# Layer 0's two attention runs joined into one pipeline, and six rows' squares at the turn streamed over weights of ones

## What is computed

```python
def _rms_norm(x, g, eps=1e-6):
    y = x * lax.rsqrt(jnp.mean(x * x, axis=-1, keepdims=True) + eps)
    return y * g
...
def _diff_attend(q, k, v, lam):          # 4 heads, two maps of width 32 per head, values of 64
    s = jnp.einsum('bhcqd,bhckd->bhcqk', q, k) * (A_DQK ** -0.5)
    p = jax.nn.softmax(s, axis=-1)
    w = p[:, :, 0] - lam * p[:, :, 1]
    return jnp.einsum('bhqk,bhkd->bhqd', w, v)
...
    yA_lat = _diff_head_out(_diff_attn_blocks(qA, kA_all, vA_all, lam), g_subln_l, lam_init)  # 1280 keys
    if last: return y_lat, None
    yA_ctx = _diff_head_out(_diff_attend(_heads_qk(pc[4]), kA_ctx, vA_ctx, lam), ...)          # 256 keys
...
        h_lat = h_lat + gf * _rms_norm(f_lat, g_post_ffn[l])       # end of layer l
        h_ctx = h_ctx + gf_c * _rms_norm(f_ctx, g_post_ffn[l])
        u_lat = _modulate(_rms_norm(h_lat, g_pre_mix[l + 1]), sm, cm)   # start of layer l + 1
```

## Time and profile before

| | us |
|---|---|
| median of three runs | 3106.45 |
| lowest, highest | 3102.74, 3108.12 |
| the profiled execution's own time | 3101.55 |
| span of the profile | 3099.8 |
| TensorE busy | 2863.0 (92%) |
| VectorE busy | 1947.9 (63%) |
| ScalarE busy | 1235.6 (40%) |
| GpSimd busy | 564.8 (18%) |

### The profile page before, as it was taken

One profiled execution on the slowest core, in us unless ns is written; L12 is line 12 of the kernel. 1 busy time (PEld: TensorE's weight loads), 2 busy tenths in 40 slices (PEclk: granted clock), 3 DMA queues, 4 the chain that ended last, 5 costly groups with the idle time before them and its releaser, 6 DMA issues.

```text
span 3099.8 us, 47110 instructions
## 1 busy us (share of the span) xinstructions
PE 2863.0 (92%) x17730; PEld 1611.3 (52%) x17730; DVE 1947.9 (63%) x2717; ACT 1235.6 (40%) x2368; POOL 564.8 (18%) x449
## 2 busy tenths in 40 slices
PE   6999887889889999999998999988889999999997
PEld 4555644654535556757755554554554444444443
DVE  5976786882575405626746687678964673374755
ACT  5112455883543213313334311448864542231332
POOL 0031010001317202102212004010003161221221
PEclk9999996999999999999999799999999999999998
DMA  6111114332142111111141311113322432111142
GB/s 242 55 35 45 28 46 139 128 134 66 55 146 74 61 41 41 43 40 55 42 150 41 142 48 41 38 49 110 114 82 88 134 118 68 48 61 49 58 150 105
DMA packets 69172, 248.95 MB, mean 80 GB/s; under 512 B 9104, under 2 KB 9872, under 8 KB 69008
## 3 DMA queue, kind: packets, MB, share of 16 engines
q1 hardware_dynamic: 67856, 241.44, 23.1%
q10 hardware_dynamic: 1152, 5.24, 0.4%
HBM read 221.75 MB, written 19.92 MB: 78 GB/s over the span
## 4 chain that ended last, share of the span: by engine, by line
PE 63%; issue 19%; DVE 11%; ACT 5%; POOL 1%; DMA 1%; SPq 0%; POOLq 0%; DVEq 0%; ACTq 0%
PE PS L831 38%; PE PS L990 18%; DVE wlo L1959 2%; PE PS L852 2%; DVE R L2138 1%; ACT whi L1454 1%; DVE R L2125 1%; PE PS L1216 1%; ACT SW L1822 1%; ACT X L1573 1%; ACT R L1571 1%; DVE X L2454 1%; PE PS L1261 1%; PE PS L1195 0%; DVE X L2098 0%
## 5 line engine op out<-in xcount | busy, mean ns | idle before, releaser
L831 PE MATMUL PS<-R,whi 128*128 128x512 f16 (+1 forms) x4992 | 1354.8, 359 | 40.3 <-DVE wlo L1959 23.4
L831 PE MATMUL PS<-R,wlo 128*128 128x512 f16 (+1 forms) x2496 | 895.4, 359 | 0.0
L831 PEld LDWEIGHTS PS<-R,whi 128*128 128x128 f16 x4992 | 489.2, 99 | 537.5 <-issue 37.9
L990 PE MATMUL PS<-R,whi 128*128 128x256 f16 (+2 forms) x2352 | 510.3, 326 | 0.0
L1959 DVE SCALAR_TENSOR_TENSOR wlo<-stage,whi 128x1024 f16<-128x1024 f32 (+1 forms) x204 | 279.0, 1368 | 358.6 <-ACT whi L1454 357.6
L831 PEld LDWEIGHTS PS<-R,wlo 128*128 128x128 f16 x2496 | 245.8, 98 | 241.3 <-issue 8.5
L990 PE MATMUL PS<-R,wlo 128*128 128x256 f16 (+2 forms) x1176 | 319.2, 326 | 0.0
L990 PEld LDWEIGHTS PS<-R,whi 128*128 128x128 f16 x2352 | 230.1, 98 | 152.0
L1454 ACT ACTIVATE whi<-stage 128x1024 f16<-128x1024 f32 (+1 forms) x204 | 210.3, 1031 | 136.6 <-PE PS L831 85.0
L2164 DVE TENSOR_REDUCE tiny<-PS 128x1 f32<-128x1280 f32 (+1 forms) x144 | 197.0, 1368 | 38.6 <-PE PS L1018 38.3
L1988 DVE TENSOR_TENSOR X<-X,PS 128x256 f32<-128x256 f32 (+2 forms) x294 | 150.8, 548 | 92.6 <-PE PS L990 92.3
(11 more groups left out here) (231 smaller groups left out, 3565.5 us busy)
## 6 DMA issues: line engine op xcount, KB each, us to landing
stage<-in_w_gu SPq DMA_DIRECT2D x120, 512.0 KB, 3.4
X<-in_w_ada SPq DMA_DIRECT2D x70, 512.0 KB, 3.3
stage<-in_w_down SPq DMA_DIRECT2D x48, 512.0 KB, 3.3
stage<-in_w_in SPq DMA_DIRECT2D x44, 512.0 KB, 3.3
stage<-in_w_out SPq DMA_DIRECT2D x32, 512.0 KB, 3.2
h_save<-R SPq DMA_DIRECT2D x24, 640.0 KB, 5.3
R<-h_save SPq DMA_DIRECT2D x24, 640.0 KB, 4.7
R<-in_w_ada SPq DMA_DIRECT2D x16, 512.0 KB, 13.2
```

The source lines that it names most:

```text
L831: last = mm(slot(into, t0, t1)[:, c0 - t0:c1 - t0], w[:, j, k, :], row, start=(k == 0 and q == 0), stop=(k == K - 1 and q == 2))
L990: last = mm(s_bank(nf, t, o, n), w[:, j, k0 + k, :], row, start=(k == 0 and x == 0), stop=(k == PAIRS - 1 and x == 2))
```

## The change

Two parts.

The two runs of layer 0's attention become one pipeline of ten tiles. `attend(l)` is called once; `tile_back` and `back` make the last context tile the one before the first latent tile, `first_tile` is true only for the first tile of the layer, and `through` counts semaphores over the border (a negative head number lies in the context run). The drain after the context run, TensorE's wait for its output and the short first latent tile are gone; the first latent scores are issued within the last context tile. Layer 1's order of work is as before. SP's and GpSimd's programs are not touched.

At the turn, `turn_sums` takes the squares of h's rows 0 to 5 as the moving operand over weights of ones (two matmuls of 512 and 256 columns a row, accumulated in PSUM where the spread goes later), which puts the sum of a token on all partitions. Rows 6 and 7 are done as before. VectorE's `turn_mean_square` waits for row 5, multiplies by the identity, reduces it to a value for each token, scales it and, when row 7 is done, adds the sums of rows 6 and 7. Besides, `keep_clock(n, 6)` issues n matmuls of 256 f16 columns into bank 6, which nothing reads: 8 behind the sums of Y (in both layers), 6 behind the first columns, 8 behind the sums of h and 16 behind the second spread. They wait for nothing.

```diff
+        SPREAD_ROWS = KD - 2
...
-        def back(r, h, n):
-            return (r, h - n) if h >= n else (r - 1, HA + h - n)
+        def per_head(name, nk):
+            return {"scores": 2, "exps": 2, "wt_ps": len(key_groups(nk)), "wt": len(key_groups(nk)),
+                    "pv": len(key_groups(nk))}.get(name, 1)
+        def first_tile(l, run, r):
+            return isinstance(r, int) and r == 0 and run == attend_runs(l)[0][0]
+        def tile_back(l, run, r):
+            return ("c", CT - 1) if run == "l" and isinstance(r, int) and r == 0 else (run, r - 1)
+        def back(l, run, r, h, n):
+            return (run, r, h - n) if h >= n else tile_back(l, run, r) + (HA + h - n,)
+        def through(l, run, name, n):
+            if isinstance(n, int) and n < 0:
+                return heads_before(l, run, name) + n * per_head(name, CT) if (l, run) == (0, "l") else None
+            return n * per_head(name, CT if run == "c" else NTILE) + heads_before(l, run, name)
...
+            def keep_clock(n, bank):
+                for _ in range(n):
+                    mm(PS[:, bank, 0:2 * P], ones16[:, 0:P], ones16[:, :], start=True, stop=True)
...
-            def end_sums(k, then=None):
+            def turn_sums(k, then):
 
                 inst, a0, a1 = STEPS[k]
-                ready, used, n = ("y_sq_ready", "y_sq_used", Y_STEPS.index(STEPS[k])) if inst % 2 else \
-                    ("h_sq_ready", "h_sq_used", H_STEPS.index(STEPS[k]))
-                rows = (0, KD - 1) if inst % 2 else range(KD)
-                for d in rows:
-                    if inst % 2 and d == 0:
-                        pe.wait_ge(S[used], (KD - 1) * n + KD - 2)
+                n = H_STEPS.index(STEPS[k])
+                for d in range(KD):
+                    pe.wait_ge(S["h_sq_ready"], KD * n + d + 1)
+                    if d < SPREAD_ROWS:
+                        at = spread_to(k)
+                        for c0, c1 in spans(a0, a1):
+                            last = mm(PSF[:, at + c0 - a0:at + c1 - a0], ones[:, :], square_row(d)[:, c0:c1],
+                                      start=(d == 0), stop=(d == SPREAD_ROWS - 1))
                     else:
-                        pe.wait_ge(S[ready], KD * n + d + 1)
-                    src = xrow(2 + d % 2 if d else 0)
+                        for x in range((a1 - a0) // P):
+                            last = mm(PS[:, 7, x:x + 1], square_row(d)[:, a0 + x * P:a0 + (x + 1) * P], ones[:, 0:1],
+                                      start=(d == SPREAD_ROWS and x == 0), stop=(d == KD - 1 and x == (a1 - a0) // P - 1))
+                    if d:
+                        last.then_inc(S["h_sq_used"], 1)
+                    then(d)
+            def end_sums(k):
+                inst, a0, a1 = STEPS[k]
+                n = Y_STEPS.index(STEPS[k])
+                for d in (0, KD - 1):
+                    if d:
+                        pe.wait_ge(S["y_sq_ready"], KD * n + KD)
+                    else:
+                        pe.wait_ge(S["y_sq_used"], (KD - 1) * n + KD - 2)
                     for x in range((a1 - a0) // P):
-                        last = mm(PS[:, 7, x:x + 1], src[:, a0 + x * P:a0 + (x + 1) * P], ones[:, 0:1],
-                                  start=(d == 0 and x == 0), stop=(d == KD - 1 and x == (a1 - a0) // P - 1))
-                    if d:
-                        last.then_inc(S[used], 1)
-                    if then:
-                        then(d)
+                        last = mm(PS[:, 7, x:x + 1], square_row(d)[:, a0 + x * P:a0 + (x + 1) * P], ones[:, 0:1],
+                                  start=(d == 0 and x == 0), stop=(d > 0 and x == (a1 - a0) // P - 1))
+                last.then_inc(S["y_sq_used"], 1)
...
-            def attend(l, run, t_first, nt, nk):
-                s, before = (lambda n: S[n]), (lambda n: heads_before(l, run, n))
-                groups = key_groups(nk)
-                NG, keys, done = len(groups), nk * P, tiles_before(l, run)
...
+                def tile(run, r):
+                    first = first_tile(l, run, r)
+                    end = isinstance(r, int) and r == runs[run][1] - 1
+                    after = ("l", 0) if run == "c" and end else (run, r + 1)
+                    last = run == "l" and end
+                    done = tiles_before(l, run)
...
-                            scores(*((r, h + 1) if h < HA - 1 else (r + 1, 0)), 0, back(r, h, 1) if h or not first else None)
+                            scores(*((run, r, h + 1) if h < HA - 1 else after + (0,)), 0, back(l, run, r, h, 1) if h or not first else None)
...
-                scores(0, 0, 0)
-                tile(0, first=True)
-                if nt > 2:
-                    with pe.Fori(1, nt - 1) as r:
-                        tile(r)
-                tile(nt - 1, last=True)
-                modulation_end(nt - 1, HA - 1)
+                nt = runs["l"][1]
+                if "c" in runs:
+                    scores("c", 0, 0, 0)
+                    for r in range(runs["c"][1]):
+                        tile("c", r)
+                else:
+                    scores("l", 0, 0, 0)
+                tile("l", 0)
+                with pe.Fori(1, nt - 1) as r:
+                    tile("l", r)
+                tile("l", nt - 1)
+                modulation_end("l", nt - 1, HA - 1)
...
-                for run, t_first, nt, nk in attend_runs(l):
-                    attend(l, run, t_first, nt, nk)
-                    pe.wait_ge(S["ot_done"], tiles_before(l, run) + nt)
+                attend(l)
+                pe.wait_ge(S["ot_done"], (l + 1) * NTILE - (CT if l == LAYERS - 1 else 0))
...
                 k = step_of(4 * l + 3, 1)
                 end_sums(k)
+                keep_clock(8, 6)
                 pe.wait_ge(S["slot_free"], unit0(l + 1, "in"))
                 spread(k)
                 if l < LAYERS - 1:
                     first_columns(l + 1, 0, KD)
-                    end_sums(k + 1, lambda d: first_columns(l + 1, KD + d, KD + d + 1))
+                    keep_clock(6, 6)
+                    turn_sums(k + 1, lambda d: first_columns(l + 1, KD + d, KD + d + 1))
+                    keep_clock(8, 6)
                     spread(k + 1)
+                    keep_clock(16, 6)
...
+                    act.wait_ge(S["wt_ps"], count(run, "wt_ps", n) + (p + 1))
+                    if p:
                         if not (isinstance(r, int) and n == 0):
 
-                            act.wait_ge(s("pv"), (NG * n + (p + 1 - (NG if p else 2 * NG))) + before("pv"))
+                            act.wait_ge(S["pv"], count(run, "pv", n - 1) + (p + 1))
+                    elif not (first_tile(l, run, r) and h < 2):
+                        act.wait_ge(S["pv"], count(run, "pv", n - 2) + 1)
...
+            def turn_mean_square(k):
+                inst, a0, a1 = STEPS[k]
+                n = (a1 - a0) // P
+                used, at = (KD - 1) * H_STEPS.index(STEPS[k]), spread_to(k)
+                spread_rows = xrow(1)[:, a0:a1].rearrange("p (t c) -> p t c", c=P)
+                dve.wait_ge(S["h_sq_used"], used + SPREAD_ROWS - 1)
+                own.link(TT(spread_rows, PSF[:, at:at + a1 - a0].rearrange("p (t c) -> p t c", c=P),
+                            ident[:, :].rearrange("p (t c) -> p t c", t=1).to_broadcast([P, n, P]), ALU.mult))
+                own.link(RED(per_tok[:, 1, 0:n], spread_rows, AX.X, ALU.add))
+                own.link(TS(per_tok[:, 1, 0:n], per_tok[:, 1, 0:n], 1.0 / D, 1e-6, ALU.mult, ALU.add))
+                dve.wait_ge(S["h_sq_used"], used + KD - 1)
+                STT(per_tok[:, 0, 0:n], PS[:, 7, 0:n], 1.0 / D, per_tok[:, 1, 0:n], ALU.mult, ALU.add).then_inc(S["mean_sq"], 1)
...
-                    inverse_root(k + 1)
+                    turn_mean_square(k + 1)
+                    diagonal(k + 1)
                     scale_rows(k + 1)
```

More of the change, by code:

```diff
@@ L1057, in token_major, with modulation @@
                     last.then_inc(S["o_ps"], 1)
-                def modulation(r, h):
+                def modulation(run, r, h):
                     for x, i in enumerate(ada_step(l, run, h)):
@@ L1652, in tile @@
                         if h or not first:
-                            wt_copy(*back(r, h, 1), 0)
-                        exps(r, h, 1)
-                per = HA
-                tile(0, first=True)
+                            wt_copy(*back(l, run, r, h, 1), 0)
+                        exps(run, r, h, 1)
+                per, nt = HA, runs["l"][1]
+                for r in range(runs["c"][1] if "c" in runs else 0):
+                    tile("c", r)
+                tile("l", 0)
                 with act.Fori(1, nt) as r:
```

307 lines of the change are left out of this document (155 added, 152 removed).

## The result

The changed kernel took 3081.07 us (median of 4 runs, 3078.61 to 3083.51) beside 3105.06 for the kernel before (3102.74 to 3108.12). The ratio is 0.9921, 95% interval [0.9909, 0.9933]: 24.5 us faster, 20.8 to 28.3. The forecast was 3089.7, a gain of 16.8. The sign and the two places were right and the size was a third too small: the time lies 0.6 us inside the low end of the stated range (3080.5), and the gain is above the 23.6 that the sum gave with every term in full. The profiled execution took 3078.61 (span 3076.8), 22.9 less than that of before.

What follows compares the result with a forecast made beforehand. TensorE, busy 92% of the span, was taken as the bound. Joint 6.0, turn 10.3 and end 0.5 gave 16.8 off the profiled 3101.55, 3084.7; the median's 4.9 carried made 3089.7 us, range 3080.5 to 3099.5.

Steps and rivals of the forecast that it cites:

- First latent maximum 12.9 earlier, less 3.7 for a full tile: Layer 0's joint: drain and refill removed, 12.9 us; a full first latent tile returns 3.7, so 9.2 saved.
- 2.1 for the lower clock and 1.1 for a quarter of a further head: Layer 0's joint: first latent head 8.1 instead of 6.0; quarter of another head's 4.4 charged; 6.0 us left saved.
- The discount of 3.2: Layer 0's joint: lower clock and quarter of a further head together, taking the saving from 9.2 to 6.0 us.
- The ring, 0.6: First latent head: second modulation unit's transfer lands at 503.0, TensorE comes at 502.4 and waits 0.6 us.
- The waits, passed over: Attention's waits: SP's transfers and GpSimd's powers said to wait on the same counts; no gain was counted.
- the premise that only joint, turn and end matter: Whole kernel: no other stage of a layer moves by over 2 us, else the premise is wrong.
- The statistic 8.0 earlier: Turn into layer 1: with streamed squares the statistic is done near 1719.3 against 1727.27, 8.0 us saved.
- The weighing of the rule: Turn's squares: rule makes twelve loads 1.28 us at either clock, little gain; the forecast went by the trace, 1.50 and 2.56.
- Fillers 2.3 and end 0.5: Matmuls over ones: 2.3 us returned at the turn's spreads and first products, 0.5 at layer 1's end.
- Rows at 1.2 GHz (1): Turn: streamed rows run at 1.2 GHz, 3.35 against 3.01 us each; total gain 4.0, 3102.4; chance 0.10.
- further heads at 1.2 GHz (2 and 3): Layer 0's joint: 1.2 GHz for two further heads, 3097.3, chance 0.10; or through two latent tiles, 3124, chance 0.04.
- a drain that stays (4): Layer 0's joint: a wait still drains the pipeline, joining brings nothing; gain 10.8, 3095.6; chance 0.06.

Runs made afterwards that it cites:

- waits alone: Kernel before with only the sums in the attention's waits reordered, so that several waits share a register: 3100.72 us, ratio 0.9987.
- fillers alone: Kernel before with only 8, 6, 8 and 16 matmuls over ones added, its squares' loads as they were: 3102.34 us, ratio 0.9996.
- loads with fillers: Kernel before, squares still as twelve loads a row, with the change's matmuls over ones and four more behind each row: 3104.68 us, ratio 1.0006.
- part B alone: Kernel before with the changed kernel's turn (streamed squares, matmuls over ones) and the attention of before: 3096.65 us, ratio 0.9978.
- less the joining: Changed kernel with layer 0's attention as two runs again, keeping the new sums in the waits and the changed turn: 3090.35 us, ratio 0.9956.
- part A alone: Kernel before with layer 0's two attention runs as one pipeline and the rewritten waits, the turn as before: 3092.88 us, ratio 0.9968.
- A with three idle: The kernel of part A alone with three small scratch-scaling instructions added to VectorE's program at the turn: 3093.16 us, ratio 0.9965 to before.
- changed, again: The changed kernel itself, unaltered, measured again on the same chip as the other runs: 3080.22 us, ratio 0.9928 to before.
- without fillers: Changed kernel without any matmul over ones: 3081.92 us, ratio 0.9934 to before.
- more fillers: Changed kernel with 12 instead of 8 matmuls over ones before the first spread and 18 instead of 8 before the second: 3080.97 us, ratio 0.9926.
- fillers in every wait: Changed kernel with matmuls over ones in every wait of the turn (16, 10, 13 and 34): 3079.71 us, ratio 0.9924 to before.
- four rows: Changed kernel with four of the eight square rows streamed instead of six, the last four as twelve loads each: 3083.74 us, ratio 0.9937.

## Why the prediction was right, and where it was not

Each profiled execution can be cut at the same events. "To tile 1" is from VectorE's first maximum of the context run to the first maximum of the second latent tile. "Attention 0" is from the same first maximum to the first product of the out-projection. "Turn" is from the start of the first spread to the first half sums of layer 1's attention (it holds unchanged work too). Then come that attention's first six pitches and its last tile. Each is a difference of two start times:

```
                        to tile 1  attention 0   turn   six pitches 1  last tile 1
before                    62.08      248.15     443.24     141.15        19.57
waits alone               61.76      244.88     443.87     140.74        17.97
fillers alone             59.97      244.06     442.57     141.18        19.57
loads with fillers        59.75      243.60     447.18     141.16        18.05
part B alone              61.79      247.49     435.02     141.10        20.89
less the joining          61.88      243.47     436.01     139.86        17.86
part A alone              52.83      237.75     443.90     140.80        17.98
A with three idle         54.04      236.40     445.63     139.92        17.86
changed                   52.74      234.73     435.96     139.83        17.85
changed, again            51.70      234.33     436.05     139.81        17.86
without fillers           51.43      233.41     436.03     139.82        17.85
more fillers              53.82      237.91     435.40     139.85        17.85
fillers in every wait     51.35      237.89     433.48     139.87        17.86
four rows                 51.53      234.83     436.25     139.88        17.86
```

What differs between the traces of before and after: attention 0 13.4, turn 7.3, layer 1's attention 1.3 and 1.7, 23.7 in all, less 0.6 at the start. But attention 0 alone varies by 4.7 between kernels that share its structure, before's execution was the longest of its six and after's below the mean of its eight. The means are 245.3 with two runs and 235.9 with one: 9.4, and of the 13.4 some 4 are how the executions fell. The 9.4 holds some of the waits' gain: the two kernels that have two runs and the new sums average 244.2, which leaves 8.3 for the joining by itself.

**First latent maximum 12.9 earlier, less 3.7 for a full tile: right.** The eight joined executions have it 28.5 to 28.7 behind the context run's first, where 28.8 was forecast. To tile 1 the means are 52.4 and 61.2: 8.8 saved, 9.34 in the compared pair, 9.2 forecast before the discounts.

**2.1 for the lower clock and 1.1 for a quarter of a further head: the step that failed.** The events came as described, 0.50 in the first head and a wait for the ring even three times as long, yet the first latent tile took 24.15, in the mean of eight 23.85 (22.82 to 25.33), which is a steady tile. The working held the first head's 8.1 against an average head of 6.0. In this kernel's steady tile the heads are uneven: 6.32, 5.60, 6.36, 5.37 (first maxima at 570.93, 577.25, 582.85, 589.21 and 594.58). The joint's were 7.44, 5.11, 6.24, 5.36. So the first lost 1.12, not 2.1, and the next two gave 0.6 of it back; the slack that the windows of the earlier trace rows had shown on both engines is the likely reason. In four of the eight the first head took only 6.1 to 6.5. No further head came at 1.2 GHz here. In two others (more fillers, A with three idle) the clock was at 0.50 again for some 6 us in the second and third head, and the second took 6.11 and 6.25 instead of 5.11: 1.1 lost, where the forecast had up to 4.4. The discount of 3.2 should have been about 0.5.

**The ring, 0.6: mis-sized, 1.81** (1.43 to 1.88 in the eight), and hidden in the same slack. What it would be worth to have the transfer earlier was not tried.

**The waits, passed over: the term that was missing.** "SP's other transfers and GpSimd's powers keep their order and wait on the same counts" was true and beside the point: the counts of the attention were summed in another order, and several waits now share a register. That is worth 4.0 (1.2 to 6.8) by the run on it, and the premise that only joint, turn and end matter was wrong for layer 1: 3.0 us moved there, over the 2 us that was named as the test. Of its pitches 0.3 to 0.4 in all goes with the waits (140.74 and 140.80 against 141.15) and 1.0 more with where VectorE's loop stands in its program, as the three idle instructions show; with the old waits, in part B alone, VectorE's longer turn gave nothing (141.10). The last tile is 17.85 to 17.98 in all ten executions with the new waits and 18.05 to 20.89 in the four without. The 18.05 is the kernel before with fillers and its old waits, so the waits alone do not settle it. Why is open.

**The statistic 8.0 earlier: right, to a tenth, step by step.** Row pitch 1.80 (1.6 to 1.84 forecast), VectorE's product and reduction 0.95 each (0.9), rows 6 and 7 at 1.00 and done 3.1 behind VectorE's last row. The streamed row took 1.56, a little over the 1.30 to 1.36; VectorE's pace hid it. In the table, three unfilled kernels with loads have a turn of 443.7 and four executions with six streamed rows and the fillers of the change 435.8: 7.9. (The fourth unfilled one, A with three idle, has 445.63, the excess in unchanged work behind the second spread.) From the first spread to the second alone it is 32.05 to 32.46 in those four with loads and 24.07 in the changed kernel, with fillers and without.

The weighing of the rule stands. Of twelve loads the same row took 1.50 at 1.00 and 2.56 at 0.50 in one timeline, with the fillers alone. The Trainium skill, page "TensorE: Matmul & The Clock Gate", section "LDWEIGHTS (loading the stationary operand)", has one formula for a load, its columns over 1.2, and names no level of the clock; read as holding at both, it gives an estimate of 1.28 for twelve. The traces agree nearly at 1.00 (1.41, the PEld line at 1703.14) and not at 0.50 (2.68 for a row's loads in the kernel before). By such a rule part B, which gained 6.8 alone, would have gained little.

**Fillers 2.3 and end 0.5: wrong, both are nothing by the traces.** Without any, the turn is 436.03 against 435.96 and 436.05. Behind the loads of rows 6 and 7 and an idle wait, the clock falls again with eight as with none (in part B alone it did not). With more of them the spreads come at 1.00, but at the turn what the spread gains is in part spent in the queue. At the end of layer 1 twelve returned 1 us where eight returned nothing. Each of these is too small for the runs to tell.

**The sum.** By the means of the traces: 9.4, 7.9, 1.3 and 1.6 to 1.7 (17.9 against the mean of 19.5 of four), 20.2. The two comparisons say 22.3 and 24.5, each give or take 4. With the last tile counted to them, the waits' part of this is 1.6 in layer 0 and 2.0 in layer 1 (0.4 and 1.6), near the 4.0 of their run. That the forecast stayed in its range is in part luck: fillers and end, counted at 2.8 and worth nothing, covered nearly half of what the joint and the waits were short. Parts A and B alone add up to 16.7, give or take 5; the 1.0 of the loop's place comes only with both, the rest of that gap is within the intervals and stays open.

**The rivals.** Rows at 1.2 GHz (1), further heads at 1.2 GHz (2 and 3) and a drain that stays (4) all fell: the streamed rows were at 1.00 in all seven kernels that have them, and all eight joined executions reached the second latent tile within 54.1 us, also the two in which the clock fell again.

## What to carry to other kernels

Charge a disturbance against that head's or step's own time in the steady state, not against the average, and let slack behind it give back before anything is deducted. When a change rewrites how a loop computes its counts, do not pass it over: no busy column shows it, and here it was worth 4.0 us. Compare the loop's register and wait instructions before and after, and give the rewriting a run of its own. A many-loads, few-columns reduction that TensorE does at its lower clock can be turned round, data streamed over fixed ones, and here that worked without any filling.

## What was not expected of the hardware

- Rows of twelve f32 loads with one-column matmuls ran at 1.00 for three rows and at 0.50 from the fourth, in three kernels that began them at 1.00 with fillers or streamed rows ahead of them; four filler matmuls between the rows (0.60 us) did not move that. In other kernels the clock fell in the second row already. Six streamed rows of 1.56 stayed at 1.00 throughout, in six kernels.
- The same loop on VectorE was 0.12 us a tile shorter with three instructions more ahead of it in the program, all of it in the one step shown. Why was not looked into.
- Executions of one kernel differ by some 13 us between lowest and highest (3096.07 to 3109.63 in 30 runs of before), and kernels that share all code up to the joint reach it between 469.6 and 473.7. One pair of traces tells the attention of layer 0 to some 4 us only, beside the 9 that were sought there. Over the fourteen executions the stretch from the second latent tile's first maximum to the last half sums went with the mean granted clock: 175.5 to 177.2 us at 1.00, 177.1 to 180.5 at 0.98 or 0.99.
